# Attention of a two-layer decoder step: six query-block groups per head pair, two score banks per head, a one-bank projection emptied by thirds

## The chip, the cores and the metric

The kernel runs on one core of one Trainium2 chip. The metric is the device time of one launch in microseconds (us). Engines: PE is TensorE, DVE is VectorE, ACT is ScalarE, POOL is GpSimd, SP issues the DMAs.

## The reference

One inference step of a trunk of two layers, for a prompt of 1024 tokens and 8 sample sequences of 4 tokens with shared weights (1056 tokens in all, D = 1024). Layer 0 mixes by convolutions, layer 1 by attention; each is followed by a gated convolutional FFN. The change concerns layer 1:

```python
q, k, v = qkv_split(rms_norm(hp, g_mix[1]), w_qkv)        # 16 heads of 64
# each head, for (window, dilation) in ((128, 1), (512, 4), (2048, 16)):
#   query t reads positions t, t - d, ..., t - window, at or above 0
s = q.k / 8 - slope_h * distance
o, lse = softmax(s) @ v, log(sum(exp(s)))
att = sum over branches of softmax(lse) * o
hp = hp + att @ w_o
# sample tokens: the same over a cache of 2048 rows and the 4 new ones
```

The kernel adds the three branches up by one table of distances: a score gets the table's bias (or -1e30), so that one softmax over all keys of a head gives the merged output.

## The kernel before, in words

Tokens lie along the free dimension, in three thirds of 352 (NT = 3, TS = 352). Big matmuls split each operand into a high and a low fp32r part and do three products, so a projection unit of 128 output columns is 3 thirds x 8 k-blocks x 3 = 72 matmuls of 352 columns.

Attention goes by pairs of heads, eight pairs (`pairs`, L519). For a pair, `QT`, `KT`, `VT` hold its projected rows; there are two sets of QT and KT. The order on each engine is written out by hand in a function `pair(pr)`, and each pair is a sequence of eight steps, one per block of 128 queries, block 7 (1024 keys) first and block 0 (128 keys) last. In a step, for both heads (hh = 0, 1):

- PE `scores` (L1051): q.k into one PSUM bank per head, 512 columns at a time, so blocks 7 to 4 take two chunks and the others one.
- DVE `neg_scores` (L2357): adds the bias table `wt`, negates into `neg_s`, with the row minimum; behind the second chunk a small reduce joins the two minima. Ahead of each, `settle` is a copy of one element.
- ACT `probs` (L1617): exp in place, with the row sum. DVE `norm` (L2378): reciprocal of the sum and scaling of `neg_s`.
- PE `turn` (L1091): transposes of 128x128 blocks, four to a bank, "lo" and then "hi" for blocks 7 to 4. DVE `turned` (L2386) copies head 0's bank, ACT `turned` (L1629) head 1's, into `pT`.
- PE `weigh` (L1103): values times transposed weights into `O`; ACT `outputs` copies `O` into `att` after four blocks.

Sample queries ride along as phases in steps 1, 3, 5 and 7 (`sample_phase`, L1140): scores against the cached keys in two parts (SP loads `kvr` from DRAM, one part ahead), exp over 928 keys in `sps`, transposes of the weights, values in two parts, and transposes of the result `so`. These phases use head 0's score bank.

PE also computes the projections of the next pair in between: `filler(n)` (L1065), 24 pieces of 9 matmuls, one k-block in all three thirds, into the three banks of `dense`. When a projection (8 pieces) is full, DVE empties it at once by `project` (L2344), 1056 columns. The weights are split high on ACT (`qkv_hi`, L497) and low on POOL (`qkv_lo`, L504). In the last pair there is no next pair; there seven pieces of 9 are k-blocks 0 to 6 of output projection unit `U_WO`, which need `att` split into `xs` by ACT (`att_hi`, L1636) and POOL (L1843).

PSUM, eight banks: `dense` = reg0 (three banks), scores `S` = reg1 banks 0 and 1, transposes `TP` = reg1 bank 2 and ob bank 0, `O` = ob bank 1.

After the last pair PE finishes `U_WO`, then `U_WO + 1` and units 2 to 7, which DVE adds to `h`, and the second FFN follows.

## Time and profile before

| | us |
|---|---|
| median of 3 runs | 2580.74 (2578.37 to 2582.78) |
| profiled execution, its own time | 2584.8 |
| its span | 2582.6 |
| PE busy | 2519.9 (98%) |
| DVE busy | 1670.5 (65%) |
| POOL busy | 969.2 (38%) |
| ACT busy | 801.2 (31%) |
| chain that ended last: PE | 87% of the span |
| chain that ended last: DVE | 7% |
| mean granted TensorE clock | 0.996 |

The span runs from the first to the last instruction; the time around it is 2.2 us. A busy PE has a matmul in flight. The attention stage lies between 1140.86 us and 1750.4 us of the span.

### The profile page before, as it was taken

What the parts mean: (1) busy time and instruction counts of PE and PEld (TensorE: products, weight loads), DVE (VectorE), ACT (ScalarE), POOL (GpSimd) and SP (SyncE); (2) the same over time, 40 slices, a digit from 0 to 9 for tenths busy, and PEclk for the clock granted to TensorE, in tenths of its full rate; (3) what the DMA queues carried; (4) which work ended last, traced back from release to release, by engine and by line L of the source; (5) the groups of instructions that cost most, each with busy time, mean ns of one, the idle gap of its engine ahead of it and who ended that gap; (6) DMA issues with size and microseconds to landing.
All of it is one profiled execution on the core that took longest, in us unless ns stands there. A gap on an engine that the chain in (4) does not pass through costs nothing.

```text
span 2582.6 us, 41756 instructions
## 1 busy us (share of the span) xinstructions
PE 2519.9 (98%) x17036; PEld 2361.7 (91%) x17036; DVE 1670.5 (65%) x2622; ACT 801.2 (31%) x1415; POOL 969.2 (38%) x650
## 2 busy tenths in 40 slices
PE   8999999999999999999999999979999999999998
PEld 8989988999999999987777777759999999999998
DVE  6999778666666655555555555564776666665556
ACT  5111443333333211333333333343423333332112
POOL 1000136777777322331001011033277777762223
PEclk9999999999999999999999999999999999999999
DMA  4111101455444644435344444333078777785222
GB/s 147 48 41 41 42 27 59 143 142 144 143 144 140 216 150 157 165 139 172 123 143 168 139 157 170 122 131 145 17 258 280 270 272 270 273 297 198 77 90 85
DMA packets 108669, 383.93 MB, mean 149 GB/s; under 512 B 24000, under 2 KB 44352, under 8 KB 106048
## 3 DMA queue, kind: packets, MB, share of 16 engines
q1 hardware_dynamic: 108480, 381.26, 43.9%
q8 instruction: 136, 2.23, 0.4%
q14 instruction: 53, 0.43, 0.1%
HBM read 339.15 MB, written 176.04 MB: 199 GB/s over the span
## 4 chain that ended last, share of the span: by engine, by line
PE 87%; DVE 7%; POOL 2%; issue 2%; ACT 2%; DMA 1%; DVEq 0%; POOLq 0%; SPq 0%; ACTq 0%
PE reg L966 28%; PE reg L825 19%; PE reg L792 10%; PE reg L1078 9%; PE ob L966 3%; PE reg L1058 3%; PE ob L1114 3%; PE reg L805 3%; PE reg L898 2%; PE reg L1031 1%; PE reg L1099 1%; PE ob L1099 1%; PE reg L1167 1%; POOL wq L1769 1%; PE reg L1154 1%
## 5 line engine op out<-in xcount | busy, mean ns | idle before, releaser
L966 PE MATMUL reg<-xo,wq 128*128 128x352 f32 x5280 | 861.9, 323 | 18.3 <-DVE tmp L2174 6.9
L966 PEld LDWEIGHTS reg<-xo,wq 128*128 128x128 f32 x5280 | 850.7, 189 | 23.3 <-DVE tmp L2174 7.5
L825 PE MATMUL reg<-hid,w_sp 128*128 128x352 f32 x3024 | 485.3, 322 | 0.0
L825 PEld LDWEIGHTS reg<-hid,w_sp 128*128 128x128 f32 x3024 | 485.0, 188 | 0.0
L489 POOL TENSOR_TENSOR w_sp<-w_raw,w_sp 128x1024 fp32r<-128x1024 f32 x63 | 174.4, 2771 | 731.0 <-ACT w_sp L484 710.5
L1905 DVE TENSOR_TENSOR h<-reg,h 128x1056 f32<-128x1056 f32 x192 | 241.3, 1257 | 259.1 <-PE reg L825 211.9
L1769 POOL TENSOR_TENSOR wq<-wqr,wq 128x512 fp32r<-128x512 f32 x168 | 240.2, 1440 | 213.1 <-DVE wqr L2134 134.6
L1769 POOL TENSOR_TENSOR wq<-w_raw,wq 128x512 fp32r<-128x512 f32 x168 | 266.5, 1598 | 60.6 <-ACT wq L1328 60.5
L1078 PE MATMUL reg<-xs,w_sp 128*128 128x352 f32 x1512 | 279.4, 331 | 0.4 <-DVE VT L2349 0.4
L1078 PEld LDWEIGHTS reg<-xs,w_sp 128*128 128x128 f32 x1512 | 240.4, 188 | 18.2 <-issue 18.1
L792 PE MATMUL reg<-xs,w_sp 128*128 128x352 f32 x1584 | 253.5, 322 | 0.5 <-DVE h L1905 0.5
L792 PEld LDWEIGHTS reg<-xs,w_sp 128*128 128x128 f32 x1584 | 252.0, 188 | 1.7 <-issue 1.7
L1328 ACT ACTIVATE wq<-wqr 128x512 fp32r<-128x512 f32 x176 | 110.7, 629 | 423.3 <-DVE wqr L2131 285.5
L507 POOL TENSOR_TENSOR w_sp<-w_raw,w_sp 128x1024 fp32r<-128x1024 f32 x21 | 50.0, 2380 | 475.6 <-ACT w_sp L502 456.8
L484 ACT ACTIVATE w_sp<-w_raw 128x1024 fp32r<-128x1024 f32 x83 | 87.9, 1059 | 425.1 <-PE reg L825 273.5
L2195 DVE SCALAR_TENSOR_TENSOR acc<-g,pt,acc 128x1024 f32<-128x1024 f32 x88 | 184.3, 2094 | 3.1
L1633 ACT ACTIVATE pT<-ob 128x512 f32<-128x512 f32 (+1 forms) x96 | 47.1, 491 | 328.9 <-PE ob L1099 328.9
L2223 DVE TENSOR_TENSOR tmp<-reg,sil 128x352 f32<-128x352 f32 x64 | 31.5, 521 | 178.4 <-POOL sil L1789 178.4
L2390 DVE COPY pT<-reg 128x512 f32<-128x512 f32 (+1 forms) x96 | 53.4, 557 | 97.5 <-PE reg L1099 97.1
L1328 ACT ACTIVATE wq<-w_raw 128x512 fp32r<-128x512 f32 x176 | 108.8, 621 | 19.7 <-DMA w_raw<-in_wstream 10.7
L2367 DVE CUSTOM_DVE_ANT_0 neg_s<-reg,wt 128x512 f32<-128x512 f32 (+1 forms) x192 | 107.3, 559 | 6.9 <-DVE eps L2355 0.3
L1626 ACT ACTIVATE neg_s<-neg_s,nmx 128x896 f32<-128x896 f32 (+7 forms) x128 | 98.1, 768 | 35.9 <-DVE nmx L2372 33.2
(264 smaller groups left out, 3082.4 us busy)
## 6 DMA issues: line engine op xcount, KB each, us to landing
w_raw<-in_wstream SPq DMA_DIRECT2D x192, 512.0 KB, 4.4
out_sv<-in_cache_v SPq DMA_DIRECT2D x16, 4088.0 KB, 17.0
out_sk<-in_cache_k SPq DMA_DIRECT2D x16, 4088.0 KB, 16.8
kvr<-in_kva SPq DMA_DIRECT2D x16, 2048.0 KB, 9.1
kvr<-in_kvb SPq DMA_DIRECT2D x16, 1536.0 KB, 7.0
hid_spill<-tmp SPq DMA_DIRECT2D x44, 528.0 KB, 5.5
hraw<-hid_spill SPq DMA_DIRECT2D x44, 528.0 KB, 4.5
wt<-in_wtab SPq DMA_DIRECT2D x16, 512.0 KB, 5.3
```

The costliest lines, as they stand in the source:

```text
L484: nc.scalar.activation(w_sp[:, u % 3, 0, :], w_raw[:, u % 3, :], ACT.Copy).then_inc(w_hi, 1)
L489: nc.gpsimd.tensor_tensor(w_sp[:, u % 3, 1, :], w_raw[:, u % 3, :], w_sp[:, u % 3, 0, :].bitcast(F32), ALU.subtract).then_inc(w_lo, 1)
L792: mm = nc.tensor.matmul(out[:, t, :], w[:, wh, k * P:(k + 1) * P], xs[:, xh, k, t * TS:(t + 1) * TS], start=(k == 0 and wh + xh == 0), sto ...
L825: mm = nc.tensor.matmul(out[:, t, :], w[:, wh, kk * 512 + m * P:kk * 512 + (m + 1) * P], hid[:, par_g, kk, xh, t * TS:(t + 1) * TS], start ...
L966: mm = nc.tensor.matmul(out, w[:, wh, k * P:(k + 1) * P], xo[:, o, 1 - xh if o == X_T3 else xh, k, :], start=(first and k == 0 and wh + xh ...
L1078: mm = nc.tensor.matmul(dense[:, t, :], w[:, wh, k * P:(k + 1) * P], xs[:, xh, k, t * TS:(t + 1) * TS], start=(k == 0 and wh + xh == 0), s ...
L1328: nc.scalar.activation(wq[:, ring(L, j, q), 0, :], quad_src(L, j, q), ACT.Copy).then_inc(wq_hi, 1)
L1626: nc.scalar.activation(neg_s[:, hh, 0:w], neg_s[:, hh, 0:w], ACT.Exp, bias=nmx[:, m, hh:hh + 1], scale=-1.0, accum_out=lsum[:, 0, hh:hh + ...
L1769: nc.gpsimd.tensor_tensor(wq[:, r, 1, :], quad_src(L, j, q), wq[:, r, 0, :].bitcast(F32), ALU.subtract).then_inc(wq_lo, 1)
L1905: nc.vector.tensor_tensor(tok(h[:, m, :]), region(r), tok(h[:, m, :]), ALU.add).then_inc(free, 1)
L2195: chain(nc.vector.scalar_tensor_tensor(out=y, in0=g, scalar=w[k], in1=y, op0=ALU.mult, op1=ALU.add))
L2367: nc.vector.tensor_tensor_reduce(out=neg_s[:, hh, lo:lo + w], in0=S[hh][:, 0:w], in1=wt[:, hh, t0:t0 + w], scale=-1.0, scalar=3.0e38, op0= ...
```

## The change

The eight steps become six groups of query blocks, (7), (6), (5), (4), (3, 0) and (2, 1). Each head has two score banks, so a group's scores are one wide region of up to 1024 columns, and the minimum of a block with more than 512 keys is one instruction; the joining reduce goes. `S` of head 0 is reg1 banks 0 and 1, `S` of head 1 is both banks of ob, `TP` is reg0 banks 0 and 1, `O` is reg1 bank 2, and `dense` is the single bank reg0 bank 2.

The filler becomes 18 pieces of 12 matmuls, four k-blocks of one third. Two pieces fill a third, which DVE then empties (`next_third`) before the next third may start. The PE order of a group is: transposes lo, piece, scores of the next group, transposes hi, piece, weighing, sample phase, piece. The sample phases write into head 0's transpose bank. In DVE's list the handling of a sample phase and of a third stands between the minimum of the next group and its scaling.

In the last pair the filler is `U_WO + 1`, k-blocks 0 to 6, third by third in groups 3 to 5 (pieces of 12 and 9); DVE copies each third into `VT` and later adds `VT` to `h`. `U_WO` is done whole behind the pair. At the start, the first scores of pair 0 are followed by its transposes, not by filler, and DVE does their minimum before it empties V. New sample keys and values get 128 rows (zeros below) in place of 32.

The core of the diff; of most functions only the new lines are shown, the old ones stand in the listing above.

```diff
--- before.py
+++ after.py
...
+GROUPS = ((7,), (6,), (5,), (4,), (3, 0), (2, 1))
+NGR = len(GROUPS)
+BLOCKS_OF = [[(512 * n + P * kb, b, kb) for n, b in enumerate(bs) for kb in range(b + 1)] for bs in GROUPS]
+NEG0 = [sum(2 * len(bs) for bs in GROUPS[:g]) for g in range(NGR + 1)]
+NNEG = NEG0[NGR]
+SAMPLE_AT = {0: 1, 1: 2, 3: 3, 4: 4}
...
-        dense = reg[0][:, :, 0:TS]
-        S = [reg[1][:, 0, :], reg[1][:, 1, :]]
-        TP = [reg[1][:, 2, :], ob[:, 0, :]]
-        O = ob[:, 1, :]
+        S = [x[:, 0:2, :].rearrange("p a b -> p (a b)") for x in (reg[1], ob)]
+        TP = [reg[0][:, x, :] for x in range(2)]
+        dense, O = reg[0][:, 2, 0:TS], reg[1][:, 2, :]
...
+            def scores(pr, g):
+                if pr.p > 0 or g > 0:
+                    pe.wait_ge(neg_ok, pr.n(NEG0[g], NNEG))
+                for n, b in enumerate(GROUPS[g]):
+                    for lo in range(0, P * (b + 1), 512):
+                        w = min(512, P * (b + 1) - lo)
+                        for hh in range(2):
+                            rows = slice(HD * hh, HD * hh + HD)
+                            mm = nc.tensor.matmul(S[hh][:, 512 * n + lo:512 * n + lo + w], QT[pr.par][rows, b * P:(b + 1) * P],
+                                                  KT[pr.par][rows, lo:lo + w], start=True, stop=True)
                 mm.then_inc(sc_full, 1)
...
+                def filler(f):
+                    half = f % 2
                     if pr.last:
+                        if f not in (9, 10, 12, 13, 15, 16):
+                            return
+                        t, half = (f - 9) // 3, (f - 9) % 3
+                        u, n = U_WO + 1, 9 * NPAIR + t
+                        w = w_sp[:, u % 3]
+                        if half == 0:
+                            pe.wait_ge(w_lo, cnt(u))
+                            pe.wait_ge(d_free, n)
+                        pe.wait_ge(x_lo, 3 * KD + (KD - 1 if half else 4))
+                        ks = range(4, KD - 1) if half else range(4)
+                    else:
+                        (x, t), n = divmod(f // 2, NT), pr.n(9 + f // 2, 9)
+                        w = w_sp[:, pr.slot(x)]
+                        if half == 0:
+                            pe.wait_ge(d_free, n)
+                            if t == 0:
+                                pe.wait_ge(aw_lo, pr.n(x + 1, 3))
+                        ks = range(4, KD) if half else range(4)
+                    for k in ks:
+                        for wh, xh in ((0, 0), (0, 1), (1, 0)):
+                            mm = nc.tensor.matmul(dense, w[:, wh, k * P:(k + 1) * P], xs[:, xh, k, t * TS:(t + 1) * TS],
+                                                  start=(k == 0 and wh + xh == 0), stop=(k == ks[-1] and half == 1 and wh == 1))
+                    if half:
                         mm.then_inc(d_full, 1)
...
+                for g in range(NGR):
+                    turn(g, "lo")
+                    filler(3 * g)
+                    if g == 0:
                         turn_values()
+                    if g == 3:
+                        turn_weights()
+                    if g < NGR - 1:
+                        scores(pr, g + 1)
                     else:
+                        turn_outputs()
+                        if not pr.last:
+                            pe.wait_ge(d_free, pr.n(9 + 6, 9))
+                            scores(Pair(pr.p + 1), 0)
+                    turn(g, "hi")
+                    filler(3 * g + 1)
+                    weigh(g)
+                    if g in SAMPLE_AT:
+                        sample_phase(SAMPLE_AT[g])
+                    filler(3 * g + 2)
...
+                for g in range(NGR):
+                    probs(g)
+                    if g == 0:
+                        if pr.p > 0:
+                            outputs(Pair(pr.p - 1), 0)
+                        if not pr.last:
+                            qkv_hi(act, pr, 1)
+                        else:
+                            act.wait_ge(d_full, 9 * NPAIR)
+                            act.wait_ge(o_free, 2 * (NPAIR - 1))
+                            act.wait_ge(ta_free, NTA * (NPAIR - 1))
+                            split_hi(act, U_WO + 1)
+                    if g == 2:
+                        act.wait_ge(sp_neg, pr.n(1, 1))
+                        nc.scalar.activation(sps[:, 0:NKEYS], sps[:, 0:NKEYS], ACT.Exp, bias=snm[:, 2:3], scale=-1.0,
+                                             accum_out=snm[:, 3:4]).then_inc(sp_exp, 1)
+                    if g == 4:
+                        outputs(pr, 1)
+                        act.wait_ge(ta_full, pr.n(ta("phase", 3) + 1, NTA))
+                        nc.scalar.activation(so[:, :, :], TP[0][:, 0:256].rearrange("p (x c) -> p x c", c=P),
+                                             ACT.Copy).then_inc(ta_free, 1)
+                    turned(g, "lo")
+                    if g == 0:
+                        act.wait_ge(tb_full, pr.n(tb("values") + 1, NTB))
                         nc.scalar.activation(vrow[:, 4:8, :], TP[1].rearrange("p (t c) -> p t c", c=P),
                                              ACT.Copy).then_inc(tb_free, 1)
+                    if g == 3:
+                        act.wait_ge(tb_full, pr.n(tb("weights") + 1, NTB))
                         nc.scalar.activation(spT[:, 4:8, :], TP[1].rearrange("p (t r) -> p t r", r=P),
                                              ACT.Copy).then_inc(tb_free, 1)
+                    if g == NGR - 1:
+                        act.wait_ge(ta_full, pr.n(ta("sample") + 1, NTA))
...
+                    turned(g, "hi")
+                    if g == 2 and not pr.last:
                         qkv_hi(act, pr, 2)
+                        act.wait_ge(d_free, pr.n(9 + 3, 9))
+                        act.wait_ge(ta_full, pr.n(ta("phase", 2) + 1, NTA))
+                        query_columns(1 - pr.par)
+                    if g == 4:
                         if pr.p < NPAIR - 2:
                             qkv_hi(act, pr, 3)
                         elif not pr.last:
+                            act.wait_ge(d_full, NT * (3 * NPAIR - 1))
                             split_hi(act, U_WO)
+                    if pr.last and g < 4:
+                        att_hi(2 * g)
+                        if g < 3:
+                            att_hi(2 * g + 1)
...
+                    if L == 1 and m == 1:
+                        chain(nc.vector.tensor_tensor(h[:, 1, :], h[:, 1, :], VT[:, :], ALU.add))
...
+            def neg_scores(pr, g):
+                dve.wait_ge(sc_full, pr.n(g + 1, NGR))
+                if g == 0:
+                    for half in range(2):
+                        dve.wait_ge(wt_in[half], pr.n(16, 16))
                 for hh in range(2):
+                    if hh == 1:
+                        if g > 0:
+                            dve.wait_ge(tb_full, pr.n(tb("hi", g - 1) + 1, NTB))
+                        elif pr.p > 0:
+                            dve.wait_ge(tb_full, pr.n(0, NTB))
+                    for n, b in enumerate(GROUPS[g]):
+                        lo, w = 512 * n, P * (b + 1)
+                        settle()
+                        nc.vector.tensor_tensor_reduce(out=neg_s[:, hh, lo:lo + w], in0=S[hh][:, lo:lo + w],
+                                                       in1=wt[:, hh, NP_ - w:NP_], scale=-1.0, scalar=3.0e38, op0=ALU.add,
+                                                       op1=ALU.min, accum_out=nmx[:, n, hh:hh + 1]).then_inc(neg_ok, 1)
...
+                def norm(g, hh):
+                    for n, b in enumerate(GROUPS[g]):
+                        dve.wait_ge(exp_ok, pr.n(neg_at(g, hh, n) + 1, NNEG))
+                        chain(nc.vector.reciprocal(lsum[:, 1, n, hh:hh + 1], lsum[:, 0, n, hh:hh + 1]))
+                        p = neg_s[:, hh, 512 * n:512 * n + P * (b + 1)]
+                        nc.vector.tensor_scalar(p, p, lsum[:, 1, n, hh:hh + 1], None, ALU.mult).then_inc(p_ok, 1)
...
+                def next_third(j):
+                    if j < 0:
+                        q, x, t = Pair(pr.p - 1), 2, 2
+                    else:
+                        q, (x, t) = pr, divmod(j, NT)
+                    if q.last or q.p < 0:
+                        return
+                    dve.wait_ge(d_full, q.n(9 + 3 * x + t + 1, 9))
+                    if x == 1 and t == 0:
+                        dve.wait_ge(kt_out, q.n(16, 16))
+                    if x == 2 and t == 0:
+                        dve.wait_ge(vt_out, q.n(16, 16))
+                    dst, r = third((QT[1 - q.par], KT[1 - q.par], VT)[x], t), third(rst, t)
+                    if x == 0:
+                        ins = nc.vector.scalar_tensor_tensor(out=dst, in0=dense, scalar=HD ** -0.5, in1=r,
+                                                             op0=ALU.mult, op1=ALU.mult)
+                    else:
+                        ins = nc.vector.tensor_tensor(dst, dense, r, ALU.mult)
+                    ins.then_inc(d_free, 1)
...
+                for g in range(NGR):
+                    for hh in range(2):
+                        norm(g, hh)
+                    if g % 2 == 0:
+                        next_third(3 * g // 2 - 1)
+                    turned(g, "lo")
+                    if g % 2 == 1:
+                        next_third(3 * g // 2)
+                    if g == 0:
+                        dve.wait_ge(ta_full, pr.n(ta("values") + 1, NTA))
                         nc.vector.tensor_copy(vrow[:, 0:4, :],
                                               TP[0].rearrange("p (t c) -> p t c", c=P)).then_inc(ta_free, 1)
+                    if g == 3:
+                        dve.wait_ge(ta_full, pr.n(ta("weights") + 1, NTA))
+                        nc.vector.tensor_copy(spT[:, 0:4, :],
+                                              TP[0].rearrange("p (t r) -> p t r", r=P)).then_inc(ta_free, 1)
+                    turned(g, "hi")
+                    if g < NGR - 1:
+                        neg_scores(pr, g + 1)
+                    elif not pr.last:
+                        neg_scores(Pair(pr.p + 1), 0)
+                    if g % 2 == 0:
+                        next_third((3 * g + 1) // 2)
+                    if g < 2:
+                        sample_scores(g)
+                    if g == 2:
                         dve.wait_ge(sp_exp, pr.n(1, 1))
                         chain(nc.vector.reciprocal(snm[:, 4:5], snm[:, 3:4]))
+                        nc.vector.tensor_scalar(sps[:, 0:NKEYS], sps[:, 0:NKEYS], snm[:, 4:5], None,
+                                                ALU.mult).then_inc(sp_ok, 1)
+                    if g == 4:
+                        dve.wait_ge(ta_full, pr.n(ta("phase", 4) + 1, NTA))
+                        dve.wait_ge(ta_free, pr.n(ta("phase", 3) + 1, NTA))
+                        nc.vector.tensor_tensor(so[:, :, :], TP[0][:, 0:256].rearrange("p (x c) -> p x c", c=P),
+                                                so[:, :, :], ALU.add).then_inc(ta_free, 1)
+                    if pr.last and g >= 3:
+                        t = g - 3
+                        dve.wait_ge(d_full, 9 * NPAIR + t + 1)
+                        dve.wait_ge(vt_out, 16 * NPAIR)
+                        nc.vector.tensor_copy(third(VT, t), dense).then_inc(d_free, 1)
...
+            neg_scores(Pair(0), 0)
+            dve.wait_ge(d_full, 3 * NT)
             project(2, reg[0][:, :, 0:TS], VT)
```

## Rows read from the trace of the kernel before

**Rows 1.** Stretches: two pairs, the second the last pair; columns in the first line.

```profile
core 0: us, PE busy (x) PEld busy (x) DVE busy (x) ACT busy (x) POOL busy (x), PEclk, DMA share, GB/s
1297.11:1374.47 77.36, 76.21 (x663) 59.46 (x661) 44.09 (x140) 26.53 (x67) 7.14 (x3) 1.00 0.44 150
1684.07:1750.40 66.33, 51.92 (x505) 34.96 (x504) 44.06 (x133) 30.42 (x64) 20.30 (x8) 1.00 0.35 117
```

**Rows 2.** PE in order of time: start, us, what, [idle before, releaser].

```profile
1310.18 1.73 PE L1078 MATMUL reg<-xs,w_sp 128*128 128x352 f32 x9
1311.84 1.92 PE L1154 MATMUL reg<-kvr,qb 128*32 128x512 f32 x16
...
1321.96 3.15 PE L1078 MATMUL reg<-xs,w_sp 128*128 128x352 f32 x18
1325.04 1.13 PE L1058 MATMUL reg<-KT,QT 64*128 64x512 f32 x4
...
1340.31 1.31 PE L1114 MATMUL ob<-pT,vrow 128*64 128x128 f32 x20 [0.46 <-DVE pT L2390]
...
1373.77 0.41 PE L1211 MATMUL reg<-ident,so 128*128 128x128 f32 x2 [0.37 <-DVE pT L2390]
```

**Rows 3.** DVE in order of time, the same pair, and a group of the page.

```profile
1308.65 0.56 DVE L2367 CUSTOM_DVE_ANT_0 neg_s<-reg,wt 128x384 f32<-128x384 f32 x1
...
1317.09 0.69 DVE L2390 COPY pT<-reg 128x512 f32<-128x512 f32 x1 [2.38 <-PE reg L1099]
1317.87 0.69 DVE L2367 CUSTOM_DVE_ANT_0 neg_s<-reg,wt 128x512 f32<-128x512 f32 x1
...
1333.36 0.55 DVE L2383 TENSOR_SCALAR neg_s<-neg_s,lsum 128x640 f32<-128x640 f32 x1
...
L2223 DVE TENSOR_TENSOR tmp<-reg,sil 128x352 f32<-128x352 f32 x64 | 31.5, 521 | 178.4 <-POOL sil L1789 178.4
```

**Rows 4.** ACT in order of time, the same pair.

```profile
1302.17 1.13 ACT L1626 ACTIVATE neg_s<-neg_s,nmx 128x1024 f32<-128x1024 f32 x1
...
1329.39 1.05 ACT L502 ACTIVATE w_sp<-w_raw 128x1024 fp32r<-128x1024 f32 x1
...
1347.60 0.21 ACT L1611 ACTIVATE qb<-QT 64x16 f32<-64x16 f32 x1
```

**Rows 5.** POOL in order of time, the same pair.

```profile
1330.52 2.38 POOL L507 TENSOR_TENSOR w_sp<-w_raw,w_sp 128x1024 fp32r<-128x1024 f32 x1 [29.15 <-ACT w_sp L502]
```

**Rows 6.** Start of the attention stage: PE, and DVE emptying V.

```profile
1140.86 1.13 PE L1058 MATMUL reg<-KT,QT 64*128 64x512 f32 x4
1142.37 1.68 PE L1078 MATMUL reg<-xs,w_sp 128*128 128x352 f32 x9 [0.38 <-DVE VT L2349]
...
1140.97 1.26 DVE L2349 TENSOR_TENSOR VT<-reg,rst 128x1056 f32<-128x1056 f32 x1 [10.33 <-PE reg L1031]
```

**Rows 7.** Landing times of the key and value loads (tile kvr).

```profile
DMA to landing us min/median/max: 6.8/8.2/12.1
```

**Rows 8.** Last pair in order of time: DVE, POOL, PE.

```profile
1717.56 2.54 DVE L2383 TENSOR_SCALAR neg_s<-neg_s,lsum 128x640 f32<-128x640 f32 x1
...
1714.64 5.11 POOL L1843 TENSOR_TENSOR xs<-att,xs 128x1056 fp32r<-128x1056 f32 x2 [3.73 <-ACT xs L1638]
...
1720.84 1.13 PE L1058 MATMUL reg<-KT,QT 64*128 64x512 f32 x4 [1.80 <-DVE snm L2400]
...
1750.69 13.37 PE L805 MATMUL reg<-xs,w_sp 128*128 128x352 f32 x81 [0.23 <-ACT att L1700]
```

**Rows 9.** PE behind two idle times elsewhere, and stretches about the first (PEclk).

```profile
1859.91 7.35 PE L966 MATMUL reg<-xo,wq 128*128 128x352 f32 x36 [3.46 <-DVE tmp L2174]
...
1856.00:1859.00 3.00, 0.45 (x3) 0.16 (x2) 2.67 (x4) 2.95 (x5) 0.00 (x0) 1.00 0.00 0
1860.00:1862.00 2.00, 2.00 (x7) 2.00 (x8) 1.97 (x3) 1.99 (x6) 0.98 (x1) 0.50 0.00 0
...
386.66 2.17 PE L966 MATMUL reg<-xo,wq 128*128 128x352 f32 x12 [3.58 <-DVE wq L2143]
```

481 lines of the change are left out of this document (167 added, 314 removed).

## The prediction

> **What bounds the kernel now.** I read first the page: PE is busy 98% of the span and 87% of the chain of waits, so only what PE does or waits for can move the time. Next the stretches of the attention stage. A head pair with filler lasts 77.36 us, in which PE is busy 76.21 [rows 1]: idle 1.15, while DVE (44.1) and ACT (26.5) are far from full. The last pair, whose filler is 7 pieces in place of 24, lasts 66.33 with 14.4 idle. So pairs 0 to 6 are bound by PE, the last by the chain scores, DVE minimum, ACT exp, DVE scaling, transposes. Then the order of time on PE: nine filler matmuls take 1.66 from their start to the next run's, eighteen in one run take 3.08 [rows 2], so a matmul costs 0.16 and each run about 0.2 on top (the pipeline is refilled). The waits inside a pair are small: 0.46 ahead of a weighing run, 0.37 ahead of the transposes of `so`, which wait for a copy of the bank [rows 2]. Adding undisturbed start-to-start distances over the pair I get 75.4; 1.95 of 77.36 is waits and what a run loses behind one.
>
> **PE work per pair (0 to 6).** The matmuls stay the same: 216 filler, 36 blocks of scores, transposes and weighing per head, the same sample phases; padding the new keys changes 32-row operands to 128 rows, not their columns, so nothing. Filler runs go from 20 (24 pieces, four of them adjacent) to 18, weighing runs from 8 to 6: four runs at 0.2 are 0.8. Score runs go from 12 to 6. The run of four takes 1.06 [rows 2], two overlapping instructions per 0.53, so a second chunk behind it may save nothing, at most 0.2: 0 to 1.2, I take 0.5. Sum 1.3 per pair. No operation of the sample phases changes its price.
>
> **Waits per pair.** The old waits go: `so` is ready long before its transposes, and a filler piece now stands between the last transposes of a group and their weighing (2.1 against a bank's copy of 0.7 [rows 3]). What is late next? At each group's end PE turns to transposes that need the scaling of the new group. From the end of "hi" DVE does: copy (0.2 to 0.6), minimum over both heads, then scaling. A 512-wide minimum takes 0.69 and a 384-wide one 0.56 [rows 3], so 1024 wide 1.22, with its small settling copy 1.35 a head. ACT's exp of 1024 is 1.15 [rows 4], scaling with its reciprocal 0.9 (0.55 for 640 columns [rows 3], so about 0.7, and 0.2). In the sixth group, with the next pair's 1024 columns, that is 0.2 + 1.35 + 1.35 + 1.15 + 0.9 = 5.0 (the second head, needed 0.5 later), and PE has piece, weighing, piece: 2.1 + 1.25 + 2.0 = 5.35: covered, with 0.3 to 0.8 to spare. In the other groups a sample phase (1.7 to 2.3) is added to the cover, but in groups 0, 1 and 4 DVE handles that phase's result BEFORE the scaling, and it can start only when the phase ends, one piece (2.0) before the transposes. Group 0: 0.14 + 0.8 (minimum 0.69 with its settling copy) + 2 x 0.87 = 2.65, due for the second head at 2.5: 0.15 late. Group 1, with the extra reduce (0.15) and one more third (0.52 [rows 3]) queued behind the scaling before the bank is free: 0.25 + 0.1. Group 4: add 0.42, four short scalings 2.0: 0.15 late. Group 2: ACT does the weight split (1.05) and eight query copies (0.11 apart, 1.1 in all [rows 4]) before exp; then POOL's split of 2.38 [rows 5] runs while DVE scales `sps`. Beside POOL a scaling is held up: 2.54 for 640 columns [rows 8], against 0.55. By my sum the scaling of group 3 ends 10.3 to 10.7 after the group's start where PE needs it at 10.5 and 11.0: 0 to 0.3. The six borders give 0.7 a pair, bounds 0 (all chains covered) and 1.95 (the old waits return in full).
> The emptying by thirds: a third of 352 columns is 0.52 [rows 3], 1.56 for three against 1.26 for one [rows 6]: DVE has that. PE needs the bank again after eight transposes (0.85) at the earliest, and DVE is done 0.65 after the piece's end. Q, K, V of the next pair are complete in time: K's last third is emptied at the start of group 4, scores of the next pair come in group 5. POOL and SP: the key and value loads keep their order; the tightest is the last one of a pair, issued at the end of phase 3 and needed 2.0 + 0.85 + 2.1 + 1.3 + 0.25 + 2.1 + 1.25 = 9.9 later, landing in 8.2 in the median (12.1 at worst [rows 7]). Hidden, I take 0.
> Gain per pair 1.3 + 1.95 - 0.7 = 2.55, over seven pairs 17.9; bounds 0.8 and 4.4 per pair, the likely ones 1.3 and 3.3.
>
> **The start.** Before, filler begins 1.51 after the first scores (1140.86 to 1142.37 [rows 6]) and hides the first softmax. Now transposes come first. Scores of both chunks end 2.2 after 1140.86; minimum of two heads to 4.95; then DVE empties V (1.26) ahead of the scaling: 6.2, first scaling 7.1, second 7.9. PE idles 5.0 and the pair starts effectively at 7.45: a loss of 5.9 (bounds 5 and 6.5).
>
> **The last pair.** Here every chain is bare. Group 0, from its first transposes: lo 1.0, values from 1.4 (behind DVE's third and copy) with head 1's from 1.9 to 2.4, scores to 4.3, hi to 5.3, head 1's copy to 6.0, weighing to 8.0, phase 1 to 9.9; DVE's sample minimum to 10.8; the scaling begun at 10.95 ends behind POOL's second `xs` part (ACT's two copies end at 8.0; POOL's 5.1 to 5.2 for two [rows 8] run from 7.0 to 12.2): 12.5. Group 1 in the same way: scores 1.35 to 3.05, hi 3.85, weighing 6.2, phase 2 8.0, minimum and reduce 9.0, scaling behind POOL (5.4 to 10.6) 11.0. Group 2, without a phase: hi 3.3, minimum to 5.5, POOL 4.8 to 10.05, scaling 10.4. Group 3: lo 1.15, piece 3.3, weights 4.2, scores 5.7, hi 6.0, then a wait to 9.95, piece of nine 11.6, weighing 12.9, phase 14.8, ACT's copy of `so` 15.3. Group 4: to phase 4 9.9, add and two scalings 12.0. Group 5 to the end of weighing 7.2. Sum 68.4, against 66.33: a loss of 2.1. Two things stand out. Group 3's second piece wants all seven low parts of `xs`, but ACT makes the seventh copy only at the end of group 3 and POOL needs 2.5 for it: PE waits 3.9 there, where the kernel before asked for that part three steps later. And while POOL makes these parts, scaling stalls, as in the row of 1717.56 with POOL at work from 1714.64; PE then idles 1.80 [rows 8]. The Trainium skill (SBUF — State Buffer, "Who interferes with whom") says that VectorE in a two-port mode and GpSimd exclude each other for the whole instruction; the row bears that out. By it groups 0 to 2 carry the 5 us that are in my sum; without it the last pair would be 63.7. Bounds 62 and 71. Behind it PE waited 0.23 and handed over in 0.3 [rows 8], which goes: +0.3. The added add of VT to h (1.26) lies under the 11.5 of a W_O unit's matmuls: 0.
>
> **The clock.** PE idled 3.46 ahead of 1859.91, at a granted clock of 1.00 up to there, and in 1860 to 1862 the clock was 0.50; the 36 matmuls behind it took 7.35 where full pace is 6.0. Behind another idle of 3.58 twelve matmuls took 2.17, which is full pace [rows 9]. The two new waits (5.0 at the start, 3.9 in the last pair) are of that length, and the old attention stage has no wait over 1.8. A stretch at 1.2 GHz like the one seen costs 1.4 each: 0 to 2.8 (more if it lasts longer), I take 2.2. The Trainium skill (TensorE: Matmul & The Clock Gate, "Why this matters for your kernels") warns of idle gaps between bursts of matmuls for this reason; by it alone both would be hit, 2.8.
>
> **Sum.** 17.9 - 5.9 - 2.1 + 0.3 - 2.2 = 8.0 less than the profiled execution's 2584.8 (span 2582.6), which lies 4.1 above the median of the runs. Of the median: 2580.74 - 8.0 = 2572.7.
>
> **The rivals.**
> A, fuller gain: no wait at the group borders (3.25 x 7 = 22.8), no clock drop: 22.8 - 5.9 - 2.1 + 0.3 = 15.1, time 2565.6. For it: DVE idles 33 us a pair, and my lateness is tenths. Against: three borders are late in my own sums.
> B, waits change place: 1.95 a pair stays. Then 9.1 - 5.9 - 2.1 + 0.3 - 2.2 = -0.8: 2581.5. For it: fewer, larger hand-overs, with one bank each for transposes and projection.
> C, slower: the chain from the end of a group's transposes to the next group's scaling becomes the bound. Its place is all six borders, whose cover in my sums is between -0.25 and +0.8. If each chain is 0.6 longer than I add up (a minimum that reads two banks in one instruction is in no row, four hand-overs cross engines), groups 0, 1, 4 pay 0.6 each and 2, 5 about 0.2: 2.2 a pair, 15.4, time 2588.1. It decides from 1.1 a pair on, where my gain is gone. Against it: cross-engine hand-overs in the profile are 0.03 to 0.06.
> D, the thirds do not do what they say: DVE reaches a third late since it stands behind scaling, and PE waits at even groups' first piece; 1 us at three places is 3 a pair, 21, time 2594. For it only the order in DVE's list; in my sums it is late by 0.1 once.
>
> **Chances.** My forecast 0.46 (own range 2567 to 2579), A 0.20, B 0.20, C 0.11, D 0.03. A run of this kernel tells 0.2%, 5.2 us, from no change: faster is below 2575.6. Of my forecast 0.36 lies there and 0.10 within; A 0.20 faster; B 0.03 faster, 0.15 same, 0.02 slower; C and D 0.12 slower, 0.02 same. Faster 0.59, same 0.27, slower 0.14. The range takes in A and B and the mild part of C: 2563 to 2585 (all of A's terms with no loss in the last pair would be 2561).
>
> **What would show it.** In the profile after: pairs 0 to 6 at 74.8 in place of 77.36, PE idle in them near 0.7 and put down to DVE's scaling; PE idle 5 ahead of the first transposes; the granted clock below 1 behind that; 3 to 4 idle in the last pair in front of the first of the short filler pieces, waiting for `xs`; the last pair at 68. Wrong if pairs stay above 76.3, if a wait for the filler bank or for keys and values shows, or if the start costs under 4.

## The result, and the profile after

| | kernel before | changed kernel |
|---|---|---|
| first comparison: median of 4 runs each | 2581.76 us (2578.37 to 2586.42) | 2555.66 (2553.09 to 2561.66) |
| second comparison: median | 2582.17 (19 runs) | 2557.92 (4 runs, 2557.58 to 2560.02) |
| profiled execution, its own time and its span | 2584.8, 2582.6 | 2561.66, 2559.9 |
| attention stage, first scores to the end of the last pair | 609.83 | 588.78 |
| a middle pair | 77.36 | 72.34 |

The ratio is 0.9905, with a 95% interval of 0.989 to 0.992, and 0.9911 (0.989 to 0.9931) the second time: 24 to 26 us faster. The prediction of 2572.7 had the sign, a third of the size, and a range (2563 to 2585) that misses by 5 to 7 us. One execution of the run with two edits below took 2727.11 us at a mean granted clock of 0.848, where the others of it have 0.994 or more; its median and its ratio leave that one out.

From the page of the changed kernel, its first lines and those of the chain of waits:

```profile
span 2559.9 us, 41443 instructions
PE 2496.5 (98%) x17036; PEld 2375.8 (93%) x17036; DVE 1628.7 (64%) x2409; ACT 804.6 (31%) x1415; POOL 969.6 (38%) x650
...
PE 90%; DVE 5%; issue 1%; POOL 1%; DMA 1%; ACT 1%; DVEq 0%; POOLq 0%; SPq 0%; ACTq 0%
```

PE is as busy as before by share, but 23 us less in all. Stretches (span; busy time of PE, PEld, DVE, ACT, POOL; PEclk): a middle pair from one turning of the values to the next, the last pair, the same from its values on, and two pieces at a low clock:

```profile
1301.39:1373.73 72.34, 72.24 (x664) 60.16 (x662) 38.95 (x114) 26.97 (x66) 7.19 (x4) 1.00 0.49 161
1660.27:1733.87 73.60, 53.93 (x501) 41.63 (x499) 36.60 (x99) 27.51 (x58) 19.64 (x8) 0.86 0.32 106
1661.74:1733.87 72.13, 52.90 (x492) 40.80 (x492) 35.47 (x97) 26.24 (x57) 19.50 (x8) 0.86 0.33 108
1151.94:1156.08 4.14, 4.14 (x17) 4.00 (x18) 1.45 (x3) 0.73 (x2) 2.80 (x1) 0.50 0.76 254
1685.30:1698.70 13.40, 9.16 (x52) 7.66 (x49) 8.57 (x14) 4.60 (x9) 5.19 (x2) 0.50 0.20 79
```

and the last pair of the kernel before from its values on:

```profile
1685.83:1750.69 64.86, 50.92 (x503) 34.66 (x501) 43.41 (x131) 29.03 (x63) 20.30 (x8) 1.00 0.34 114
```

Against [rows 1], idle time in a pair fell from 1.15 to 0.10, yet the pair is 5.0 shorter: most of the gain is in time that both profiles count as busy. So I took each PE instruction's start to the next one's start and added these distances up by kind, over one middle pair (77.37 and 72.33). A run is a row of matmuls of one kind with nothing of another kind between them:

| distances on PE, us | before | after | change | predicted |
|---|---|---|---|---|
| filler, 216 matmuls | 38.17 in 20 runs | 37.01 in 18 | -1.16 | -0.4 |
| scores | 10.46 in 12 | 8.95 in 6 | -1.51 | -0.5 |
| weighing | 9.07 in 8 | 8.77 in 6 | -0.30 | -0.4 |
| sample phases | 7.70 | 7.29 | -0.41 | 0 |
| transposes, with the waits ahead of their successors | 11.97 | 10.31 | -1.66 | -1.25 |

Scores in order of time on PE, after (each instruction is shown singly; `reg` and `ob` are the two heads' banks), behind them transposes, filler and a late border (the change from one group to the next, where PE turns to transposes that need the new group's scaling; here eight of them take 1.09 to the next start):

```profile
1315.91 0.69 PE L1070 MATMUL reg<-KT,QT 64*128 64x512 f32 x1
1315.91 0.69 PE L1070 MATMUL ob<-KT,QT 64*128 64x512 f32 x1
1316.44 0.59 PE L1070 MATMUL reg<-KT,QT 64*128 64x512 f32 x1
1316.45 0.59 PE L1070 MATMUL ob<-KT,QT 64*128 64x512 f32 x1
1316.87 0.38 PE L1070 MATMUL reg<-KT,QT 64*128 64x256 f32 x1
1316.88 0.38 PE L1070 MATMUL ob<-KT,QT 64*128 64x256 f32 x1
1317.09 0.38 PE L1070 MATMUL reg<-KT,QT 64*128 64x256 f32 x1
...
1317.40 0.55 PE L1123 MATMUL reg<-ident,neg_s 128*128 128x128 f32 x3
...
1325.61 1.32 PE L1123 MATMUL reg<-ident,neg_s 128*128 128x128 f32 x8
1326.70 2.18 PE L1101 MATMUL reg<-xs,w_sp 128*128 128x352 f32 x12
```

A couple is one instruction for each of the two heads, side by side. The first couple of 512 columns takes 0.53, the next 0.43; of the two of 256 columns the first takes 0.22 and the last, up to the transposes, 0.31. So columns cost 0.43 per 512 and a run 0.2 on top, half of it at either end. The row [rows 2] that I had read (1.06 for two couples, "0.53 each") is exactly 2 x 0.43 + 0.2: the fixed part was in it.

PE in order of time in the changed kernel, at the start and in the last pair:

```profile
1145.09 0.69 PE L1070 MATMUL reg<-KT,QT 64*128 64x512 f32 x1
...
1151.94 1.97 PE L1123 MATMUL reg<-ident,neg_s 128*128 128x128 f32 x8 [4.86 <-DVE neg_s L2410]
1153.56 3.33 PE L1101 MATMUL reg<-xs,w_sp 128*128 128x352 f32 x12
...
1672.59 1.45 PE L1123 MATMUL reg<-ident,neg_s 128*128 128x128 f32 x8 [2.50 <-DVE neg_s L2410]
1683.34 1.39 PE L1123 MATMUL reg<-ident,neg_s 128*128 128x128 f32 x8 [2.71 <-DVE neg_s L2410]
1694.79 1.97 PE L1123 MATMUL reg<-ident,neg_s 128*128 128x128 f32 x8 [3.67 <-DVE neg_s L2410]
1706.06 3.01 PE L1101 MATMUL reg<-xs,w_sp 128*128 128x352 f32 x9 [3.84 <-POOL xs L1866]
...
1724.79 0.66 PE L1123 MATMUL reg<-ident,neg_s 128*128 128x128 f32 x4 [1.96 <-DVE neg_s L2410]
```

They answer to [rows 6] and [rows 8]: 4.86 at the start (forecast 5.0), 3.84 for `xs` (3.9), three borders at 2.5 to 3.7. Behind the wait of 4.86 the granted clock is 0.50 (1.2 GHz), and in the last pair it is 0.50 in three stretches: 1685.2 to 1698.8 (behind 2.71, and with 3.67 in it), 1705.7 to 1709.1 (from the end of the 3.84 on) and 1726.2 to 1729.5 (behind 1.96). Behind the wait of 2.50 it stays 1.00, as it does in the whole of the old attention stage. DVE and POOL in order of time ahead of the border of 1694.79:

```profile
1689.71 2.41 DVE L2484 TENSOR_SCALAR sps<-sps,snm 128x928 f32<-128x928 f32 x1
1692.23 2.50 DVE L2410 TENSOR_SCALAR neg_s<-neg_s,lsum 128x640 f32<-128x640 f32 x1
1694.84 0.55 DVE L2410 TENSOR_SCALAR neg_s<-neg_s,lsum 128x640 f32<-128x640 f32 x1
...
1689.20 5.19 POOL L1866 TENSOR_TENSOR xs<-att,xs 128x1056 fp32r<-128x1056 f32 x2 [6.33 <-ACT xs L1665]
```

Marks at the turning of the values give the whole stage: first scores to first values 4.18, then 11.64 (+7.46); six periods of 77.38 against 72.33 (-30.3); the seventh 76.52 against 71.02 (-5.5); from there to the end of the last pair 64.86 against 72.13 (+7.27). Sum -21.1, the difference of the two stages.

### The profile page after: what moved, and what is told of

It reads as the page before. It is cut to its first block, busy times and chain, and to the rows that moved or that the text cites. A ratio compares the mean times of both kernels' runs of the same rounds, so it can differ in the third digit from the quotient of the medians.

```text
span 2559.9 us, 41443 instructions
## 1 busy us (share of the span) xinstructions
PE 2496.5 (98%) x17036; PEld 2375.8 (93%) x17036; DVE 1628.7 (64%) x2409; ACT 804.6 (31%) x1415; POOL 969.6 (38%) x650
## 4 chain that ended last, share of the span: by engine, by line
PE 90%; DVE 5%; issue 1%; POOL 1%; DMA 1%; ACT 1%; DVEq 0%; POOLq 0%; SPq 0%; ACTq 0%
PE reg L976 30%; PE reg L835 19%; PE reg L802 10%; PE reg L1101 10%; PE ob L976 3%; PE reg L1123 3%; PE reg L1070 3%; PE reg L1137 3%; PE reg L908 2%; PE reg L815 2%; PE reg L1041 1%; PE reg L1193 1%; PE reg L1180 1%; PE ob L882 1%; DVE xo L2118 1%
## 5 line engine op out<-in xcount | busy, mean ns | idle before, releaser
L1101 PE MATMUL reg<-xs,w_sp 128*128 128x352 f32 x1575 | 290.3, 334 | 3.8 <-POOL xs L1866 3.8
L1101 PEld LDWEIGHTS reg<-xs,w_sp 128*128 128x128 f32 x1575 | 254.3, 192 | 15.2 <-issue 11.0
L802 PE MATMUL reg<-xs,w_sp 128*128 128x352 f32 x1584 | 253.5, 322 | 0.1
L802 PEld LDWEIGHTS reg<-xs,w_sp 128*128 128x128 f32 x1584 | 252.0, 188 | 1.4 <-issue 1.4
L1660 ACT ACTIVATE pT<-reg 128x512 f32<-128x512 f32 x96 | 47.0, 490 | 246.0 <-PE reg L1123 246.0
L2418 DVE COPY pT<-reg 128x512 f32<-128x512 f32 x96 | 53.2, 555 | 102.4 <-PE reg L1123 101.1
L1123 PE MATMUL reg<-ident,neg_s 128*128 128x128 f32 x576 | 89.8, 285 | 18.2 <-DVE neg_s L2410 16.0
```

Source lines behind the costliest of these rows:

```text
L802: mm = nc.tensor.matmul(out[:, t, :], w[:, wh, k * P:(k + 1) * P], xs[:, xh, k, t * TS:(t + 1) * TS], start=(k == 0 and wh + xh == 0), sto ...
L1101: mm = nc.tensor.matmul(dense, w[:, wh, k * P:(k + 1) * P], xs[:, xh, k, t * TS:(t + 1) * TS], start=(k == 0 and wh + xh == 0), stop=(k == ...
L1123: mm = nc.tensor.transpose(TP[hh][:, i * P:(i + 1) * P], neg_s[:, hh, off:off + P], ident[:, :])
```

## The experiments

Times are medians; "pair" is the period in the middle of the profile, which lies between 72.31 and 72.35 in both profiles of the changed kernel (but for the first pair of the second, 72.73, whose start is at the low clock), so it tells more than a median with its 2 to 4 us of scatter.

**The changed kernel again.**

> The changed kernel, unedited, once more. Under question is whether the middle pairs repeat (72.3 us from one turning of the values to the next, 77.4 in the kernel before), and how much of the rest is one execution's chance: in the first profile the product matmuls of the second FFN were 158.9 ns apart against 161.1 in the kernel before, though both kernels run the same program there. Theory 1 (the gain is in the pairs, 35 us, less 7.5 at the start and 7.3 in the last pair): pairs at 72.3 again, start 7.4, last pair 73.6 with waits of 3.8 for xs; the FFN's rate is free to differ. Theory 2 (the pairs' rate is itself one execution's luck): pairs between 72.3 and 75.

Measured 2557.92. Pairs 72.33; first scores to first values 12.14 (more of it at the low clock); from the last values to the end 70.79 in place of 72.13. There the low clock fell on other instructions: PE is busy 51.20 in it in place of 52.90, with much the same waits (one of 4.96 in place of 3.67). Theory 1 holds.

**Scores in two runs.**

```diff
                     turn(g, "lo")
+                    scores(pr, g + 1, (0,))
                     filler(3 * g)
...
-                        scores(pr, g + 1)
+                        scores(pr, g + 1, (1,))
```

> The changed kernel with the scores of a group in two runs again, the first chunk (or first block) ahead of the filler piece, the second behind it: twelve score runs a pair in place of six, the same matmuls. Theory 1 (each further run on PE costs 0.2 to 0.25 wherever it lies, and my figure of 0.5 a pair for the merging was too small): the pair goes from 72.3 to 73.6 to 73.9, the kernel 9 to 11 us slower than the changed one. Rival, as the prediction had it (a second chunk behind the first saves nearly nothing): 72.6 to 72.8, 2 to 4 us slower.

Measured 2578.06, 0.9986 of before (0.9974 to 0.9999). The stretch of a middle pair of this run:

```profile
1304.49:1379.48 74.99, 74.83 (x663) 59.83 (x661) 38.94 (x114) 27.10 (x66) 7.15 (x3) 1.00 0.48 156
```

and PE in order of time in it:

```profile
1339.10 1.03 PE L1126 MATMUL reg<-ident,neg_s 128*128 128x128 f32 x8
1340.06 0.69 PE L1072 MATMUL reg<-KT,QT 64*128 64x512 f32 x1
```

+2.66 a pair, more than either theory: 0.44 for each further run. The score distances are +1.30 (0.22 a run). The rest is a second price that I had not thought of: eight transposes take 0.79 to 0.85 ahead of filler and 0.96 ahead of scores, so this change of kind costs 0.17, and six of them 1.0; the late borders grow by that too (1.05 to 1.23). PE is "busy" throughout (74.83 of 74.99). The kernel before had such changes at three of its steps. So this order of the scores takes back 20 of the 24 us: at 0.22 a run, 9 of them are for the splitting, the rest mostly for the place behind the transposes. It is not the order of the kernel before, which split the scores too but had the first part of each behind filler, so the 20 us are not what the merging gained.

**Filler cut into sixes.**

```diff
-                    filler(3 * g)
+                    if pr.last:
+                        filler(3 * g)
+                    else:
+                        filler(3 * g, (0,))
...
+                    if not pr.last:
+                        filler(3 * g, (1,))
```

The second half stands behind the scores.

> The changed kernel with the first filler piece of each group cut into 6 + 6 matmuls, the second half behind the scores: 24 filler runs a pair in place of 18, the same matmuls. Theory 1 (a filler run costs more than the 0.2 of the prediction, since both of its edges cost when the neighbour is a tiled run of scores: 0.25 to 0.4 a run): the pair goes to 73.8 to 74.7, 10 to 16 us slower. Rival (0.2 a run, as predicted): 73.5, 8 us slower. Second rival (runs cost nothing, waits did): 72.3.

Measured 2574.46, pair 74.94: just above the theory's 73.8 to 74.7, and by another cause. PE and DVE in order of time in group 3 of this run:

```profile
1339.55 1.23 PE L1102 MATMUL reg<-xs,w_sp 128*128 128x352 f32 x6
1342.08 0.42 PE L1124 MATMUL reg<-ident,neg_s 128*128 128x128 f32 x2 [1.31 <-DVE spT L2476]
...
1340.82 0.53 DVE L2459 TENSOR_TENSOR KT<-reg,rst 128x352 f32<-128x352 f32 x1 [4.01 <-PE reg L1102]
1341.26 0.68 DVE L2476 COPY spT<-reg 128x512 f32<-128x512 f32 x1
```

The cut delays the third; DVE, in its fixed order, takes the third first and the bank's copy behind it, and PE waits. That is 1.4 of the 2.6, and a like wait in group 5 is 0.6. So I cut only the pieces whose third is not complete with them:

```diff
+                    cut = g % 2 == 0 and not pr.last
+                    filler(3 * g, (0,) if cut else (0, 1))
```

> The first filler piece of groups 0, 2 and 4 alone cut into 6 + 6 matmuls around the scores: three more filler runs a pair, and no third of the projection is full later than before, so DVE's order gains no wait. In the run with all six pieces cut, six more runs cost 2.6 a pair, of which the traces put 1.4 and 0.6 on two transposes that waited for a bank behind a third that DVE had to empty first. Theory (a further filler run beside scores costs 0.1 itself): the pair goes from 72.33 to 72.6 or 72.7, about 2 us slower in all. Rival (it costs the 0.44 of the sum, 2.6 over six): 73.6, 9 us slower.

Measured 2560.56, pair 72.47: +0.14 for three runs, 0.05 each. F6 + F6 takes 2.22 in place of 2.10, and transposes behind filler 0.06 less than behind scores. The theory's 0.1 is still too much. The filler's gain of 1.16 is therefore not "two runs at 0.2": twelve filler matmuls take 2.01 ahead of transposes and 2.10 ahead of scores or weighing; in the kernel before nine take 1.53 ahead of transposes and 1.64 ahead of scores, weighing or samples. The old order had 16 of 20 runs end the dear way, the new one 9 of 18: 7 x 0.09 = 0.6, two runs 0.2; some 0.3 of it I can't place.

**New keys on 32 rows.**

```diff
-                        for t in range(4):
+                        for t in range(4 - hh):
...
+                        if hh == 1:
+                            mm = nc.tensor.transpose(TP[1][0:NS, 3 * P:4 * P], sps[:, NKEY:NKEYS], ident[:, :])
...
-                                    mm = nc.tensor.matmul(out[r, x * P:(x + 1) * P], spT[:, 7, r], vnew[:, :],
+                                    mm = nc.tensor.matmul(out[r, x * P:(x + 1) * P], spT[0:NS, 7, r], vnew[0:NS, :],
```

> The changed kernel with the padding of the new keys alone undone: their transposed weights and their values stand on 32 rows, not on 128. Theory 1 (operands of 32 rows cost PE an extra, at the sixteen matmuls and at the switch to and from them): 0.4 a pair, 72.3 to 72.7, 3 us slower. Rival (the prediction's: nothing): 72.3, no difference.

Measured 2563.26, pair 72.73: +0.40, the theory's number, and all of it in the sample phases (7.70 in place of 7.29). PE in order of time, fourth sample phase, in the changed kernel:

```profile
1356.25 0.86 PE L1193 MATMUL reg<-kvr,spT 128*32 128x128 f32 x24
1356.93 0.40 PE L1199 MATMUL reg<-vnew,spT 128*32 128x128 f32 x8
1357.15 0.84 PE L1193 MATMUL reg<-kvr,spT 128*32 128x128 f32 x24
```

and in this run:

```profile
1354.88 0.86 PE L1195 MATMUL reg<-kvr,spT 128*32 128x128 f32 x24
1355.67 0.42 PE L1201 MATMUL reg<-vnew,spT 32*32 32x128 f32 x8
1356.03 0.86 PE L1195 MATMUL reg<-kvr,spT 128*32 128x128 f32 x24
```

Eight matmuls go by in 0.22 (1356.93 to 1357.15) with 128 rows and in 0.36 with 32, and the 24 ahead of them in 0.68 and 0.79 (before the same as here: 0.79, 0.35).

**Scores ahead of filler.**

```diff
                     turn(g, "lo")
+                    if g < NGR - 1:
+                        scores(pr, g + 1)
...
                     filler(3 * g)
```

> The changed kernel with the scores of the next group ahead of the first filler piece, not behind it: the same runs, other neighbours. Twelve filler matmuls take 2.10 ahead of scores or weighing and 2.01 ahead of transposes, while eight transposes took 0.79 ahead of filler and 0.96 ahead of scores in the run with split scores. Theory 1 (each change of kind has its own price, 0.17 from transposes to scores, 0.09 from filler to scores): 0.08 more at each of six places, the pair at 72.8, 3 us slower. Rival (only the number of runs counts): 72.3, no difference.

Measured 2578.24, pair 75.07, +2.74; both theories missed. The distances give 1.0 for six changes from transposes to scores, as above, and most of the rest for waits: with the scores gone from there, turning of values, weights and `so` is followed at once by transposes into the same banks, which wait for their copy (0.44 idle on a DVE copy twice, 0.69 on an ACT copy once). The theory had priced the edges and forgotten the cover.

**Scaling first.**

```diff
-                    for hh in range(2):
-                        norm(g, hh)
...
                     if g % 2 == 0:
                         next_third((3 * g + 1) // 2)
...
+                    for hh in range(2):
+                        if g < NGR - 1:
+                            norm(pr, g + 1, hh)
+                        elif not pr.last:
+                            norm(Pair(pr.p + 1), 0, hh)
                     if g < 2:
                         sample_scores(g)
```

> The changed kernel with DVE's scaling of the next group moved ahead of what DVE makes of the sample phase (minimum of the sample scores, addition to so). Theory (the 0.73 a pair by which the transposes of groups 1, 2 and 5 start late is DVE's order of work, nothing else): the pair goes from 72.33 to 71.6, all seven 5 us less, and the last pair, where the same order is bare, loses 1.5 to 3 of its 73.6. Rival (the late transposes are paid by PE anyway, in switches between kinds of matmuls): pair unchanged at 72.3, last pair alone shorter.

Measured 2556.30. The stretch of a middle pair of this run:

```profile
1293.58:1365.14 71.56, 71.56 (x664) 60.21 (x661) 39.61 (x114) 26.98 (x66) 7.18 (x4) 1.00 0.49 162
```

-0.77, idle zero: the three late borders (1.04, 1.09 and 0.99 where 0.79 is free) were DVE's order and are all that was left of waits. The last pair went the other way, 74.84 from its values on. DVE, ACT and PE in order of time in it:

```profile
1658.64 2.52 DVE L2407 TENSOR_SCALAR neg_s<-neg_s,lsum 128x896 f32<-128x896 f32 x1
...
1654.31 2.05 ACT L1665 ACTIVATE xs<-att 128x1056 fp32r<-128x1056 f32 x2
1656.26 1.03 ACT L1653 ACTIVATE neg_s<-neg_s,nmx 128x896 f32<-128x896 f32 x1
...
1662.10 1.94 PE L1123 MATMUL reg<-ident,neg_s 128*128 128x128 f32 x8 [3.76 <-DVE snm L2428]
```

ACT's copies for `xs` stand ahead of exp, exp ahead of the scaling, and now the sample minimum stands behind that too.

**xs earlier.**

```diff
                     probs(g)
+                    if pr.last:
+                        for m in {1: (0, 1, 2), 2: (3, 4), 3: (5, 6)}.get(g, ()):
+                            att_hi(m)
```

> The changed kernel, in the last pair alone: ACT makes the high parts of xs behind the exps of the coming group and not ahead of them, three, two and two of them in groups 1, 2 and 3, so the seventh is there a group earlier and POOL's low parts run beside transposes and not beside DVE's scaling. Theory (the 3.8 wait for xs, the three stalled scalings of 1.39, 2.41 and 2.50 and the half clock behind those waits are the last pair's loss): 73.6 goes to 64 to 68, 6 to 9 us less. Rival (only the wait for xs goes, the stalls move): 69.5 to 70.5.

Measured 2555.17; 69.31 from the last values to the end, 1.5 to 2.8 less than in the two profiles of the changed kernel. The wait for `xs` is gone; three parts in a row on POOL (7.94) ran into the scaling, which took 2.18 and 2.65, and PE waited 3.29 and 2.10. The rival's cause holds, the stalls moved; in its count of the pair, which starts 1.5 earlier, this is 70.8, just above its 70.5.

**The start.**

```diff
-            scores(Pair(0), 0)
+            def first_scores():
+                pe.wait_ge(d_free, 2 * NT)
+                scores(Pair(0), 0)
+            pe.wait_ge(d_free, NT)
+            project(U_QKV + 2, reg[0], midway=first_scores)
...
+                    if pr.p + g == 0:
+                        filler(0)
                     turn(g, "lo")
...
-            neg_scores(Pair(0), 0)
             dve.wait_ge(d_full, 3 * NT)
             project(2, reg[0][:, :, 0:TS], VT)
+            neg_scores(Pair(0), 0)
```

> The changed kernel with the first pair's first scores issued in the middle of V's projection, V emptied before their minimum, and the first filler piece ahead of the first transposes (for the first pair alone). Theory (the start is a bare chain of 6.9 from the first scores to the first transposes, of which PE idles 4.86 and then runs at the granted clock of 0.5): two waits of about 1.3 are left, no half clock, from the end of V's projection to the first values 8.3 in place of 11.9: 3 to 4 less, and up to 3 more for the clock, 4 to 6 us in all. Rival (the half clock comes with any wait here): 2.5 us less.

Measured 2559.97. The stretch from the end of V's projection to the first values is 7.0 (11.6 and 12.1 in the changed kernel), but the first scores, 1.9, have only moved out of it into the projection. From the middle of K's projection to the first values, with the same matmuls in it, it is 26.82 against 29.26 and 29.76: 2.4 to 2.9 less. There are three waits; PE in order of time:

```profile
1142.97 2.19 PE L1098 MATMUL reg<-xs,w_sp 128*128 128x352 f32 x12 [1.42 <-DVE VT L2379]
1146.54 0.66 PE L1120 MATMUL reg<-ident,neg_s 128*128 128x128 f32 x4 [1.38 <-DVE neg_s L2415]
1147.87 0.66 PE L1120 MATMUL reg<-ident,neg_s 128*128 128x128 f32 x4 [0.67 <-DVE neg_s L2415]
```

and no low clock behind them. In the medians this can't be seen: the last pair (73.67 from its values on) and the program behind it (831.4 from the end of the stage to the end of the span; 826.0 and 829.6 in the changed kernel) took it back.

**Together**, with one `xs` part in group 0 and two each in groups 1 to 3, directly behind `probs(g)`. This order of the parts is another than in the run "xs earlier", and it was not run alone:

```diff
                             split_hi(act, U_WO + 1)
+                            att_hi(0)
+                    if pr.last and 0 < g < 4:
+                        att_hi(2 * g - 1)
+                        att_hi(2 * g)
```

> The changed kernel with three edits together: scaling ahead of the sample work (pairs at 71.56 when alone), the first scores in V's projection with the first filler piece ahead of the first transposes (7.0 from the end of V's projection to the first values when alone, against 11.6 and 12.1), and in the last pair xs parts made behind the exps, one in group 0 and two each in groups 1 to 3. Alone, two of these gained little in the whole: scaling first made PE wait 3.76 twice in the last pair, since ACT's exps stood behind its copies for xs, and three parts in one group ran into the scaling. Theory (the waits of the last pair are the order on ACT and POOL; with exps first and two parts a group a border costs 1 to 1.5 in place of 2.5 to 3.7, and the half clock there mostly goes): 5.4 in the pairs, 4.5 at the start, last pair near 63, together 18 to 20 us less than the changed kernel: 2537 to 2541. Rival (stalls and half clock only change place in the last pair, as in the runs before): 10 to 11 less, 2547.

> As the run before, without the edit of the start. Theory (the start's edit is worth its 4.6 on its own, and up to 3 for the half clock behind the wait of 4.86): 4.6 to 7 us slower than the run before. Rival (the start gains nothing in the whole, as the run with that edit alone suggests, 2560.0 against 2557.9): the same time.

Measured 2531.18 (0.981 of before, 0.9793 to 0.9827), and 2538.60 without the start's edit (0.9831, 0.9811 to 0.9851). So the three edits are 26.7 less than the changed kernel, 49 less than the kernel before. Stretches of the run with all three, a middle pair and the last one from its values on:

```profile
1291.87:1363.41 71.54, 71.54 (x662) 60.20 (x661) 39.63 (x114) 26.99 (x66) 7.14 (x4) 1.00 0.50 162
1648.30:1701.69 53.39, 45.11 (x492) 34.49 (x492) 30.47 (x97) 26.76 (x57) 19.09 (x8) 1.00 0.43 146
```

and the three largest waits of its last pair, PE in order of time:

```profile
1658.65 1.06 PE L1120 MATMUL reg<-ident,neg_s 128*128 128x128 f32 x8 [1.12 <-DVE snm L2433]
1667.46 1.06 PE L1120 MATMUL reg<-ident,neg_s 128*128 128x128 f32 x8 [0.96 <-DVE snm L2433]
1674.00 1.31 PE L1120 MATMUL reg<-ident,neg_s 128*128 128x128 f32 x8 [1.51 <-DVE neg_s L2412]
```

53.39 where the changed kernel took 72.13 and 70.79, with the same 492 matmuls (the theory's "near 63" was for the whole pair, which is 54.9 here): no wait over 1.51, no scaling held up, clock 1.00 throughout. By these marks the last pair gives 17.4 to 18.7, the pairs 5.2 to 5.6 and the start 2.4 to 2.9, in all 26. The theory's causes hold, its size for the last pair was too small.

The start is the least certain part. The medians of the two runs differ by 7.4. Their profiles differ by 2.4 up to the first values (26.82 and 29.25 from the middle of K's projection), not at all from there to the end of the stage (553.20 in both), and by 4.5 behind it, where both run the same program (827.2 and 831.7). So the edit is worth 2.4, and that it does more is not shown.

**The kernel before again.**

> The kernel before, unedited, for a second profile of it. The attention stage explains 21 us of the 24 to 26 between the two kernels; the rest lies behind it, where both run the same program but for one addition: from the last transposed weights' end to the program's end 824.6 in the one profile of the kernel before, 816.5 to 824.1 (mean 820) in eleven profiles of the changed kernel and its variants. Theory (chance of one execution): this time 817 to 822. Rival (the changed kernel really gains some 4 us behind the attention stage): 824 or more again. Pairs at 77.37 and the attention stage at 609.8 in both.

Measured 2578.57 against 2581.78 of its own repetition. Pairs 77.38, attention stage 610.05 against 609.83, and behind it 827.9 against 831.9. The expectation's numbers leave out 7.3 of that part in every run, so the 827.9 stands for its 820.6: the theory. The product stage of the second FFN as a stretch, in this profile:

```profile
1836.03:2311.17 475.14, 467.24 (x2911) 464.17 (x2910) 321.67 (x437) 159.47 (x279) 331.48 (x258) 1.00 0.73 256
```

and in the first one of the same kernel:

```profile
1833.56:2312.93 479.37, 472.03 (x2912) 469.33 (x2910) 320.73 (x437) 159.44 (x279) 331.02 (x258) 1.00 0.73 254
```

## Why the prediction was wrong

**The step that failed** is "PE work per pair", 1.3. Measured 3.8: the five rows of the table give 5.04, less the 1.2 of waits below. The 2.5 that it is too small are, over seven pairs, 17.5 of the 17.9 us by which the pairs' gain (35.8 in place of 17.9) was too small. The upper bound failed with it: 0.8 for the runs, at most 1.2 for the scores and at most 1.95 for the waits give 3.95 a pair (the prediction's 4.4 does not come out of its terms), and measured are 5.04. In it:
- "a second chunk behind it may save nothing ... I take 0.5": 1.5 in the scores, and 0.5 more where the old order had scores behind transposes. I read a rate out of a run of two couples, in which rate and fixed part can't be told apart; the chunks of 384 and 256 columns in the same pair would have parted them.
- "four runs at 0.2 are 0.8": 1.16 and 0.30, sum 1.5. The 0.2 was one number for prices that depend on the neighbour.
- "padding ... so nothing": 0.41, from the 32-row form, shown by undoing it alone.

**Waits per pair**: 1.95 before, 0.7 after. The 1.95 is the prediction's own sum; the row of the transposes fits it, since 1.66 less the 0.5 for changes of kind leaves 1.2 for the waits that went. Right: with scaling first the pair loses 0.77, at just the borders I had named for groups 0, 1 and 4 (a group's end is the next one's start), and the thirds, the keys and values and `so` cost nothing in the pairs.

**The start**: loss 5.9 forecast, PE idle 5.0. Measured 7.46 with 4.86 idle; 1.9 of it is clock (eight transposes and twelve filler matmuls took 4.79 at 0.50, 2.85 at full), so 5.5 without.

**The last pair**: loss 2.1, less 0.3 behind it. Measured 7.27, about what the clock cost. Its PE busy time from the values on is 52.90, and 45.11 for the same 492 matmuls in the version with no low clock: 7.8 for the clock. The rows give the same: in the three stretches at 0.50 PE is busy 9.40, 3.01 and 3.39, together 15.8, and half of that is 7.9. How much of it the waits would have taken up at full clock is open; between the two profiles of the changed kernel 1.70 less busy time went with 1.34 less in all. What is left, -0.5, is two larger terms: PE idles 5.3 more than in the old last pair (19.2 and 13.9), and is busy 5.8 less at full clock (45.1 and 50.9). So the 1.8 forecast for the chains was too dear, and what the clock took was left out of it. The waits for `xs` and the scaling beside POOL stood where they were said to. The rule of the Trainium skill (SBUF — State Buffer, "Who interferes with whom"), that the two exclude each other for a whole instruction, is borne out again: 2.50 where a scaling of that size is 0.55, and none held up where POOL's parts ran beside transposes.

**The clock**: 2.2 forecast for two stretches, about 9.7 paid (1.9 at the start, 7.8 in the last pair). I had counted only the waits of 5.0 and 3.9; the border waits of 2.7 and 3.7, which I had in my sums as durations, came with the longest low stretch, and the one of 1.96 with another.

**Sum of the stage**: 35.8 - 5.5 + 0.5 - 9.7 = 21.1. So two terms of the prediction were far too small, and with opposite signs: the work of the pairs by 17.5 and the clock's cost by 7.5. That the forecast missed the stage by 13 and not by 18 is luck. The medians differ by 26 and 24, with intervals that start at 21 and 18, so the stage alone can be the whole change. That the other 3 to 5 us are scatter is likely and not shown: from the end of the stage to the end of the span it took 831.9 and 827.9 in two profiles of the kernel before and 826.0 and 829.6 in two of the changed one.

**The rivals**: A (no waits) had the right direction for the wrong reason. B, C and D are out: no wait took the others' place in the pairs. None of them held that the cost of work itself, or of the clock, was misjudged, and so the range, built from their ends, was too narrow.

## What to carry to other kernels

Where PE is busy all the time, its order of kinds of matmuls is itself a cost: put equal ones together, read a run's fixed part from two lengths of run, and count changes of kind (here 0.05 to 0.17 us each, and 0.22 for each further run of scores) by start-to-start distances, not by busy time. When two parts of a chain are bare, an edit of one alone may be eaten by the other and by the clock: scaling first, alone, gained 5.4 in the pairs and lost 2.7 to 4.0 in the last pair, and the edit of the start, worth 2.4 to 2.9 by its marks, was lost in the medians. Together with another order of the `xs` parts they gave 27. That order was not run alone, so how much of the last pair's 17 to 19 is its own and how much needs the scaling first stays open. A cut or a move has a price at its edges and another in the cover that it takes from a bank's copy.
